# Five places of one encoder kernel reordered: latents' low parts, rotary sums on GpSimd, a tile ahead of values, the sixth output group in the last norm, the last chunk added by VectorE

## What is computed

```python
# MLA
c_q, c_kv, k_r = jnp.split(h @ w_in, [256, 384], axis=-1)
c_q, c_kv = rmsnorm(c_q, q_norm), rmsnorm(c_kv, kv_norm)
q = (c_q @ w_uq).reshape(B, S, 8, 128 + 64)
q_rope = rope(q_rope, cos, sin); k_rope = rope(k_r, cos, sin)
s = q_nope . k_nope + q_rope . k_rope;  p = softmax(s * scale);  o = (p @ v) @ w_o
# HGRN2
q, z_fw, z_bw, i, g = jnp.split(h @ w_in, 5, axis=-1)
o = scan(fw) + scan(bw)                       # gated scans, heads of 128
o = (rmsnorm(o, out_norm) * silu(g)) @ w_o
# around each sub-layer
x = x + rmsnorm(sublayer(rmsnorm(x, g_pre)), g_post)
```

## Time and profile before

| | us |
|---|---|
| median of three runs | 2028.69 |
| lowest and highest run | 2027.84 and 2033.7 |
| the profiled execution, its own time | 2032.39 |
| its span, first to last instruction | 2030.6 |
| TensorE busy | 2020.4 |
| VectorE busy | 925.3 |
| ScalarE busy | 714.4 |
| GpSimd busy | 676.0 |

### The profile page before, as it was taken

How to read it: one execution, slowest core, us unless ns; L and a number is a source line. 1 busy time by engine, 2 the same in 40 slices (tenths; PEclk the granted TensorE clock), 3 DMA queues, 4 the chain that set the end, 5 groups by cost and what they waited for, 6 DMA issues and landing times.

```text
span 2030.6 us, 28406 instructions
## 1 busy us (share of the span) xinstructions
PE 2020.4 (100%) x11182; PEld 1676.7 (83%) x11182; DVE 925.3 (46%) x1228; ACT 714.4 (35%) x971; POOL 676.0 (33%) x310
## 2 busy tenths in 40 slices
PE   9999999999999999999999999999999999999999
PEld 7888888888888888888888888888888878888887
DVE  6433421588474343115534311476766766433212
ACT  5222232455342222224222222465655543222221
POOL 4444444220224444442544444200000024444444
PEclk9999999999999999999999999999999999999999
DMA  4233234200223223333232333222221122322332
GB/s 166 93 98 98 91 96 133 95 22 1 63 83 98 99 93 94 99 96 104 78 99 93 96 94 103 81 86 81 68 69 64 64 73 94 99 98 93 96 96 88
DMA packets 54516, 179.49 MB, mean 88 GB/s; under 512 B 6048, under 2 KB 10400, under 8 KB 54432
## 3 DMA queue, kind: packets, MB, share of 16 engines
q1 hardware_dynamic: 54000, 176.73, 27.4%
q10 hardware_dynamic: 432, 1.57, 0.2%
HBM read 176.18 MB, written 2.10 MB: 88 GB/s over the span
## 4 chain that ended last, share of the span: by engine, by line
PE 95%; DVE 2%; ACT 1%; issue 1%; DMA 0%; SPq 0%; DVEq 0%; ACTq 0%
PE psum L637 28%; PE psum L638 28%; PE psum L639 28%; PE psum L793 2%; PE psum L794 1%; PE psum L799 1%; PE psum L1055 1%; PE psum L1162 1%; ACT prob L1666 0%; PE psum L825 0%; PE psum L822 0%; PE psum L1242 0%; PE psum L1199 0%; PE psum L1220 0%; PE psum L1241 0%
## 5 line engine op out<-in xcount | busy, mean ns | idle before, releaser
L563 POOL TENSOR_TENSOR w_lo<-raw,w_hi 128x1024 fp32r<-128x1024 f32 (+1 forms) x276 | 648.9, 2353 | 1302.6 <-ACT w_hi L1459 1302.6
L637 PE MATMUL psum<-xg_hi,w_hi 128*128 128x512 f32 x1735 | 683.4, 394 | 1.0 <-DVE xg_lo L2300 0.5
L639 PE MATMUL psum<-xg_hi,w_lo 128*128 128x512 f32 x1735 | 676.5, 390 | 0.0
L638 PE MATMUL psum<-xg_lo,w_hi 128*128 128x512 f32 x1735 | 676.3, 390 | 0.0
L1459 ACT ACTIVATE w_hi<-raw 128x1024 fp32r<-128x1024 f32 (+1 forms) x332 | 343.1, 1037 | 839.8 <-DMA raw<-w_up 464.1
L637 PEld LDWEIGHTS psum<-xg_hi,w_hi 128*128 128x128 f32 x1735 | 326.2, 188 | 71.2 <-issue 1.6
L639 PEld LDWEIGHTS psum<-xg_hi,w_lo 128*128 128x128 f32 x1735 | 326.2, 188 | 68.5
L638 PEld LDWEIGHTS psum<-xg_lo,w_hi 128*128 128x128 f32 x1735 | 326.3, 188 | 67.1 <-issue 1.2
L637 PE MATMUL psum<-hid_hi,w_hi 128*128 128x512 f32 (+1 forms) x726 | 278.0, 383 | 0.0
L638 PE MATMUL psum<-hid_lo,w_hi 128*128 128x512 f32 (+1 forms) x726 | 277.7, 383 | 0.0
L639 PE MATMUL psum<-hid_hi,w_lo 128*128 128x512 f32 (+1 forms) x726 | 277.7, 383 | 0.0
(11 more groups left out here) (258 smaller groups left out, 1617.0 us busy)
## 6 DMA issues: line engine op xcount, KB each, us to landing
raw<-w_up SPq DMA_DIRECT2D x172, 512.0 KB, 3.5
raw<-w_down SPq DMA_DIRECT2D x64, 512.0 KB, 3.5
raw<-w_hgrn SPq DMA_DIRECT2D x48, 512.0 KB, 3.5
raw<-w_down SPq DMA_DIRECT2D x32, 384.0 KB, 3.1
raw<-w_mla SPq DMA_DIRECT2D x16, 512.0 KB, 3.5
raw<-w_up SPq DMA_DIRECT2D x16, 128.0 KB, 4.6
xt<-x_t SPq DMA_DIRECT2D x8, 256.0 KB, 4.8
out<-xt SPq DMA_DIRECT2D x16, 128.0 KB, 1.7
```

The source lines that it names most:

```text
L563: pool.tensor_tensor(w_lo[slot][:, 0:n], raw[slot][:, 0:n], w_hi[slot][:, 0:n].bitcast(F32), ALU.subtract).then_inc(w_ready, 1)
L637: first = pe.matmul(ps, w_hi[slot][:, at:at + n], hi, start=start, stop=False)
L638: pe.matmul(ps, w_hi[slot][:, at:at + n], lo, start=False, stop=False)
L639: return first, pe.matmul(ps, w_lo[slot][:, at:at + n], hi, start=False, stop=stop)
```

## The change

Five places are edited.

- Latents: VectorE makes the low parts of latents 0 and 1 ahead of norming latent 2. TensorE waits for two low parts ahead of the head groups, and for the third ahead of the scores and the values.
- Rotary sums: three of the four sums move to GpSimd, between its splits of tiles 9 and 10.
- Entry of HGRN2: ScalarE's high part of a tile goes ahead of the first `values_out`, VectorE's split of tile 9 ahead of the second v_raw.
- Last quarter: `cross_keys(n, 16)` goes ahead of `o_hi(5)`, `normed_output(n - 1, 1)` behind `update(n, 8)`. The sixth output group takes bank 2 beside the ring: heads 0 to 5 go ahead of output step 6, head 6 behind it, head 7 behind step 7.
- End: chunk 7 is no more summed by GpSimd and TensorE. VectorE multiplies it and adds it to xt itself, on both sides.

```diff
-                pe.wait_ge(chunk_ready, chunk.next(MLA_LORA))
+                pe.wait_ge(chunk_ready, chunk.next(MLA_LORA - 1))
+                latent_ready = chunk.next()
...
+                lora_normed(0)
+                lora_normed(1)
+                lora_low(0)
+                lora_low(1)
+                lora_normed(2)
+                lora_low(2)
...
+                        if t == ENTRY + EXTRA + 4:
+                            for j, crossed_part in ((1, t_a), (2, t_b), (3, t_d)):
+                                pool.wait_ge(drained, GROUPS_BEFORE_MLA + evicted_up_to(MLA_ROPE + HEADS // 2 + j))
+                                pool.wait_ge(q_rotated, j)
+                                pool.tensor_tensor(q_rope[:, j, :], q_rope[:, j, :], crossed_part[:, :],
+                                                   ALU.add).then_inc(q_rotated, 1)
                         split()
...
-                    if i == 1:
-                        rotated(1)
...
-                    if i % TB == TB - 1 and i // TB + 2 < HEADS // 2:
-                        rotated(i // TB + 2)
...
                 out_of_psum.more += PAIR
+                hi_part()
                 values_out(0, 0)
-                hi_part()
                 values_out(0, 1)
...
                 first_level(0)
+                split(s, t + 3)
                 evict_value(0, 1)
                 keep(0, 0)
-                split(s, t + 3)
...
                 o_hi(4)
+                cross_keys(n, 16)
                 o_hi(5)
-                cross_keys(n, 16)
...
-                normed_output(n - 1, 1, TAIL_BANKS[0])
                 keep(n, 4)
                 update(n, 8)
+                normed_output(n - 1, 1, TAIL_BANKS[0])
...
                 o_statistics(n, (1,), TAIL_BANKS[1])
+                step_beside(fifth, fifth_slot, (5,))
+                sixth_slot = open_tile(by_dve=True)
+                bank_free.more += 1
+                pe.wait_ge(unit_out, UNITS)
+                sixth = psum[:, SIXTH_BANK, :]
                 pe.wait_ge(recip_made, recips.next())
                 widen_o(n, 0, TAIL_BANKS[0])
-                fifth_step(5)
+                step_beside(sixth, sixth_slot, (0, 1))
                 pe.wait_ge(recip_made, recips.next())
                 widen_o(n, 1, TAIL_BANKS[1])
+                step_beside(sixth, sixth_slot, (2, 3, 4, 5))
                 output_step(6, tiles, banks)
-                fifth_step(6)
+                step_beside(fifth, fifth_slot, (6,))
+                step_beside(sixth, sixth_slot, (6,))
                 output_step(7, tiles, banks)
-                fifth_step(7)
+                step_beside(fifth, fifth_slot, (7,))
+                step_beside(sixth, sixth_slot, (7,))
                 pe.wait_ge(o_moved, 1)
-                project()
                 project()
                 project(by_dve=False)
...
-                    for j in range(KB):
+                    for j in range(KB - 1):
                         dve.scalar_tensor_tensor(y[:, j, at], y[:, j, at], gains_of(s, j), psum[:, FINAL_WIDE[side], at],
                                                  ALU.mult, ALU.mult).then_inc(y_scaled, 1)
+                    j = KB - 1
+                    dve.tensor_tensor(t_a[:, at], y[:, j, at], psum[:, FINAL_WIDE[side], at], ALU.mult).then_inc(dve_step, 1)
+                    dve.wait_ge(dve_step, step.next())
+                    dve.scalar_tensor_tensor(xt[:, j, at], t_a[:, at], gains_of(s, j), xt[:, j, at],
+                                             ALU.mult, ALU.add).then_inc(x_last, 1)
```

More of the change, by code:

```diff
@@ L544, in _ @@
             for j in range(KB):
-                sp.wait_ge(x_added, j + 1)
+                if j < KB - 1:
+                    sp.wait_ge(x_added, j + 1)
+                else:
+                    sp.wait_ge(x_last, 1)
                 sp.dma_start(out[j, :, SIDES[0]], xt[:, j, SIDES[0]]).then_inc(stored, 16)
-            for n, (by_pool, by_pe) in enumerate(zip(SUMMED_BY_POOL, SUMMED_BY_PE)):
-                sp.wait_ge(x_added, KB + n + 1)
+            for n, by_pool in enumerate(SUMMED_BY_POOL):
+                if n == len(SUMMED_BY_POOL) - 1:
+                    sp.wait_ge(x_last, 2)
+                    sp.dma_start(out[KB - 1, :, SIDES[1]], xt[:, KB - 1, SIDES[1]]).then_inc(stored, 16)
+                sp.wait_ge(x_added, KB - 1 + n + 1)
                 sp.dma_start(out[by_pool, :, SIDES[1]], xt[:, by_pool, SIDES[1]]).then_inc(stored, 16)
-                sp.wait_ge(x_out, n + 1)
-                sp.dma_start(out[by_pe, :, SIDES[1]], xt[:, by_pe, SIDES[1]]).then_inc(stored, 16)
+                if n < len(SUMMED_BY_PE):
+                    sp.wait_ge(x_out, n + 1)
+                    sp.dma_start(out[SUMMED_BY_PE[n], :, SIDES[1]], xt[:, SUMMED_BY_PE[n], SIDES[1]]).then_inc(stored, 16)
             sp.wait_ge(stored, 16 * 2 * KB)
@@ L598, in _ @@
                                            ALU.subtract).then_inc(made_ready, 1)
-                    for _ in range(ENTRY + EXTRA, MLA_TILES):
+                    for t in range(ENTRY + EXTRA, MLA_TILES):
+                        if t == ENTRY + EXTRA + 4:
[4 more added lines that the diff above has]
+                                                   ALU.add).then_inc(q_rotated, 1)
                         split()
@@ L1362, in hgrn, with step_beside @@
                 bank_free.more += 1
[L1364 to L1368, removed]
+                def step_beside(ps, slot, heads):
+                    for h in heads:
+                        o_hi = xg_hi[:, h, :] if h else o_first[:, 0, :]
+                        o_lo = xg_lo[:, h, :] if h else o_first[:, 1, :]
+                        first, last = mm3(ps, (slot, h * P, P), o_hi, o_lo, h == 0, h == HEADS - 1)
                     if h == HEADS - 1:
@@ L1371, in fifth_step @@
                         last.then_inc(group_done, 1)
-                fifth_step(0)
-                fifth_step(1)
+                step_beside(fifth, fifth_slot, (0, 1))
                 turn_keys(n, 0)
                 turn_keys(n, 1)
-                fifth_step(2)
+                step_beside(fifth, fifth_slot, (2,))
                 keys_by_values(n, 0)
                 keys_by_values(n, 1)
-                fifth_step(3)
+                step_beside(fifth, fifth_slot, (3,))
                 values(n, 0)
@@ L1937, in bank @@
                     return psum[:, ENTRY_BANKS[n], :]
-                if n == fifth[0]:
-                    entry_n[0] += 1
-                    return psum[:, FIFTH_BANK, :]
+                if fifth[0] is not None and n in (fifth[0], fifth[0] + 1):
+                    beside = n == fifth[0]
+                    if not beside:
+                        entry_n[0] += 2
+                    return psum[:, FIFTH_BANK if beside else SIXTH_BANK, :]
                 return psum[:, LONG_RING[(n - entry_n[0]) % len(LONG_RING)], :]
@@ L2104, in mla, with lora_normed @@
                 reciprocals(2 * TB, TB)
-                for j in range(MLA_LORA):
+                def lora_normed(j):
                     if j != 1:
@@ L2109, in mla, with lora_low @@
                     dve.wait_ge(chunk_new, new.next())
-                for j in range(MLA_LORA):
+                def lora_low(j):
                     dve.wait_ge(chunk_hi, chunk_h.next())
@@ L2176, in mla @@
                     if j == 0:
-                        rotated(0)
+                        dve.tensor_tensor(q_rope[:, j, :], q_rope[:, j, :], crossed_part[j][:, :], ALU.add).then_inc(q_rotated, 1)
+                        dve.wait_ge(q_rotated, 1)
                 stack_lo(0)
```

17 lines of the change are left out of this document (9 added, 8 removed).

## The result

The changed kernel takes 2034.21 us (median of 17 runs, 2031.57 to 2037.03) where the kernel before, run as often beside it, takes 2029.81 us (2027.2 to 2033.7). The ratio is 1.0024 [1.0017, 1.0031]: slower by 4.4 us by the medians and 4.9 by the ratio, which lies inside the 0.3% that the prediction called no change; the interval leaves out 1, so the loss is small but real. The forecast was +2.7 us.

A forecast was written before the change was run, and what follows sets the result against it. TensorE was taken as the bound, busy 2020.4 of 2030.6 us, so only its standing time could be won. Terms +0.3 - 1.05 - 0.37 + 0 + 3.2 + 0.2 + 0.4 = +2.7 on 2028.69 gave 2031.4 us; range 2026.0 to 2035.0.

The forecast's parts named there:

- A: Latents: the wait before the first head group goes (-0.85), one at the second head's bank replaces it; +0.3 us net.
- B: Rotary sums: attention's waits go (-1.3 us), GpSimd's sums delay the first scores (+0.25); -1.05 us, between -1.3 and -0.85.
- C: Entry of HGRN2: a tile split ahead of values removes the wait for its low part; -0.37 us, bounds 0 and -0.45.
- D1: Last quarter, third quarter's norm: masked 16's wait goes, but output step 3 still waits for o_low(3); 0 us, +-0.2.
- D2: Last norm, sixth group moved forward: the output-emptying chain shifts and post_statistics waits; +3.2 us, bounds -1.2 and +3.6.
- E: Last chunk: VectorE's added instruction meets GpSimd's sums and may delay the second side; +0.2 us, bounds 0 and +0.5.
- clock: TensorE at half clock behind post_statistics after about 3 us of standing; +0.4 us taken, bounds 0 and +1.7.
- The rival by which every wait goes: Second head's bank free and outputs emptied in time, so no wait replaces those removed; -3.7 us, 2025.0, chance 0.13.
- the clock rival: After the new wait TensorE runs two stretches at 1.2 GHz, 3.4 us on top of +2.7; 2034.8, chance 0.10.
- the main case: The forecast itself for the whole kernel, median 2031.4 us, stated as 2029.5 to 2033.5; chance 0.67.

The follow-up runs named there:

- experiment 6: Changed kernel with the latents' low parts in the order of before, so head groups wait for all three latents; one run, 2037.63 us.
- experiment 9: Changed kernel with the last chunk summed as before, GpSimd and TensorE adding chunk 7; one run, 2033.18 us.
- experiment 7: Changed kernel with r_pre and scaled(t_a) made ahead of the third latent's high and low part, and tile 5's split moved ahead of the roots; one run, 2029.96 us.
- experiment 3: Changed kernel, but VectorE copies output j + 1 before adding the square of output j; 2032.54 us, ratio 1.001 to the kernel before.
- experiment 4: Changed kernel with the running sum of squares kept in a PSUM bank; 2028.9 us against 2029.84 for the kernel before, ratio 0.9996.
- experiment 10: Changed kernel with copies ahead, sums in PSUM, rope key's banks emptied first and third rotary sum later, sixth group kept; 2026.24 us, ratio 0.9981 to the kernel before.
- sixth alone: Kernel before with only the sixth output group's part of the change added; 2035.31 us, ratio 1.0028 to the kernel before.
- third sum later: Changed kernel with GpSimd's third rotary sum placed behind its split of tile 10; one run, 2033.89 us.
- experiment 1: Changed kernel with the sixth output group put back behind the seventh output; 2028.68 us against 2028.96 for the kernel before, ratio 0.9995.
- experiment 11: Changed kernel with the rope key's banks emptied first and third rotary sum later, but sixth group and output projection as before; 2026.15 us, ratio 0.9989 to the kernel before.
- experiment 5: Changed kernel with six idle 256-column matmuls ahead of the gated layers' post_statistics; 2032.9 us, ratio 1.0015 to the kernel before.

## Why the prediction came out as it did

**Where time is won and lost** was as forecast: the six stretches hold all of it but the -0.44 accounted for above. By term, with what was measured:

| term | forecast | measured | from |
|---|---|---|---|
| A, latents | +0.3 | +0.43 | -0.83 and +1.26, experiment 6 |
| B, rotary sums | -1.05 | -1.15 | +0.52 and -1.67 |
| C and D1 | -0.37 | -0.04 | stretch of before and after, see below |
| D2, sixth group | +3.2 | +3.2 | 29.78 - 26.57 |
| E, last chunk | +0.2 | -0.1 | experiment 9 |
| clock | +0.4 | +2.0 | below |
| sum | +2.7 | +4.3 | |

**A.** The wait moved to the second head, as forecast, and was 1.0 us with its hidden part where the working gave 1.0 (12.55 less 11.55). The slips behind it, for which the prediction had 0 to 0.5 and took 0.15, came to 0.28 (0.43 less 0.15). Experiment 7 shows that the bank binds, not the low parts.

**B.** All of attention's waits went, and 0.37 us beyond the 1.3 that I had counted in them. The price was also higher: q_stack grew by 0.99 us, of which 0.5 reached TensorE, against the 0.25 taken and 0.45 as the bound. The Trainium skill (Perfetto Trace Analysis, Optimizing Scalar/DVE Operations) says that such a move might not help, by which B would have been 0; here it won 1.15 us, and without the clash 1.5.

**C and D1.** The wait of the earlier trace rows is gone, and a small one for the next w_lo came some 6 us further on (0.17 us idle before the weight load at 1357.32). In D1 the wait for q_lev shrank from 0.66 to 0.32, and the one for xg_lo that I had put behind it now shows as 0.85. The two parts together moved the stretch from the first diagonal block to the last statistics of o from 273.23 to 273.19 us. That pair alone says little: in the eleven profiles with both parts it is 272.66 to 273.19, 272.87 in the mean, in the two without (before, and the sixth group alone) 273.23 and 272.97. So the two parts win about 0.2 us and not the 0.37. D1 has no share in it: from the statistics of o ahead of the last quarter to the next ones are 44.2 us, in the mean, with it and without, as forecast.

**D2.** The largest term was right in place and size, because it was a chain of other engines with a slack of 0.3 us, and work put ahead of its start moved all of it. The rival by which every wait goes (2025.0) failed at just this point. Experiments 3, 4 and 10 settle what makes the chain long: take the splits' hold on the additions away and it is 3.7 us shorter; take only the hand-over away and it is 1.7 shorter; take both away and it is 7.4 shorter. The prediction had some 4 us for the first of these, and concluded that TensorE would then set the end and 1.2 us be won. The length was right, the conclusion was not: in experiment 4 the wait before tile 46 stayed (1.71 us shown), and the stretch was 26.98 us against 26.57, 0.4 longer; only with both edits (experiment 10) was it 24.97, 1.6 shorter. The Trainium skill (SBUF — State Buffer, Who interferes with whom) says that an instruction of VectorE with two SBUF inputs contends with GpSimd's reads, and one with at most one such input, outside the two-port modes, doesn't. The trace agrees on both: 1.27 to 2.48 us for the one beside splits, 0.70 for the other.

**E.** The added instruction met a GpSimd sum on both sides. On the first it began 0.14 us ahead of the sum and took 0.48 us, the sum 0.92 instead of 0.72; on the second the sum had begun 0.29 us ahead of it, and it took 0.72 us itself. Nothing behind either was late.

**The clock** is the step that was mis-sized. I saw that the new wait lies ahead of statistics of one column, gave the half-clock stretch +0.4 in the sum and held two stretches for a rival with 0.10. The profiles of all kernels, by the wait for sqsum (us shown), the half clock behind the statistics, and the way from there to the first chunk added:

| kernel | wait | at half clock | to first chunk |
|---|---|---|---|
| changed | 2.9 | 10.2 | 374.87 |
| sixth alone | 2.8 | 6.8 | 373.75 |
| copies ahead | 2.9 | 6.8 | 373.57 |
| latents undone | 3.0 | 6.8 | 373.76 |
| third sum later | 3.2 | 10.2 | 374.93 |
| key emptied first | 2.9 | 3.4 | 372.39 |
| last chunk undone | 2.9 | 6.8 | 373.72 |
| wait filled | 0.4 | 3.4 | 372.16 |
| before | none | 0 | 371.55 |
| sixth undone | none | 3.4 | 372.28 |
| sums in PSUM | none | 3.4 | 372.25 |
| all mended | none | 0 | 371.51 |
| mended, no sixth | none | 0 | 371.54 |

The seven with the wait average 373.86 us (372.39 to 374.93), the five with none 371.83 (371.51 to 372.28), "wait filled" left out: +2.0 us for the clock. That is what I should have had in the sum; the rival's 3.4 is the bad end, which the profiled execution of the changed kernel comes near, with three stretches at half and not two. A stretch cost less than the 1.7 us at which I had it: 3.32 us for three. That the wait is the cause rests on this: with it 3.4 to 10.2 us at half clock followed, and removing it (experiments 1, 4, 10 and 11) never left more than 3.4. Filling it with matmuls (experiment 5) does not prove it, since an unfilled wait also came with 3.4 us. What decides between 3.4, 6.8 and 10.2 us from one kernel to the next with the same wait stays open.

With +2.0 the terms give +4.3 us (+4.1 with -0.2 for C and D1); the medians differ by 4.4. The median, 2034.21, is inside the stated range, but above the 2033.5 that bounded the main case and nearer to the clock rival's 2034.8, to which I had given 0.10 (and which counts the +0.4 a second time). So the places of the waits were right, and the chances on the clock were not. The absolute forecast, 2031.4, missed by 2.8: 1.6 is the clock, 0.1 the other terms, and 1.1 that the first three runs of before had a median of 2028.69 and seventeen have 2029.81. The difference between the two profiled spans, 2.0 us, would mislead: before's own profile lost 3.2 us at half clock ahead of the heads.

## What to carry to other kernels

Before moving work ahead of a chain that another engine runs, find the chain's start and its slack at the end: here 3.6 us of matmuls against 0.3 of slack came back as a wait of 3. Price such a wait with what the clock does behind it, not only by its length. And where an accumulation on VectorE runs beside GpSimd and a bank of PSUM is free, keep the running sum there.

## What the runs showed of the hardware

- An addition of 128x512 on VectorE takes 0.69 us alone and 1.27 to 2.48 beside a GpSimd split when both operands are in SBUF, and ends 0.55 us after the split; with the running sum in PSUM it takes 0.70 under three splits in a row, and the splits keep their 2.40 to 2.42 us. I had not thought of that way out.
- A sum of 128x512 costs GpSimd 1.28 to 1.30 us, and 1.55 when it begins during an instruction of q_stack. Of the two that overlap, the one that began first kept its time (q_stack's first 0.69 us) and the later one was longer (the sum 1.55, then q_stack's second 1.67 instead of 0.69).
- About 3 us of standing ahead of one-column statistics was followed by 3.4 to 10.2 us of TensorE at half clock, in seven profiles, and cost 0.9 to 3.4 us over the 371.5 of a way with none; without the standing, five profiles had 0 to 3.4 us at half clock.
